# Four activation buffers moved by 8 bytes within each SBUF partition

## The reference

```python
def swiglu(h, w_in, w_out):
    gate, up = jnp.split(h @ w_in, 2, axis=-1)
    return (jax.nn.silu(gate) * up) @ w_out
...
    for l in range(DEPTH):
        x = x + FFN_HALF * swiglu(rmsnorm(x, ffn1_norm[l]), ffn1_w_in[l], ffn1_w_out[l])
        x = x + hybrid_mixer(rmsnorm(x, mix_norm[l]), w_in[l], ...)
        x = x + FFN_HALF * swiglu(rmsnorm(x, ffn2_norm[l]), ffn2_w_in[l], ffn2_w_out[l])
...
    x = x + jnp.sum(gates * proj, axis=2) @ w_o
    x = x + jnp.square(jax.nn.relu(rms_norm(x, g_ffn) @ w_up)) @ w_down
```

## Time and profile before

| | before |
|---|---|
| median of 3 runs | 2320.74 us (2320.18 to 2322.78) |
| the profiled execution | 2317.76 us |
| its span, first to last instruction | 2316.0 us |
| granted TensorE clock, mean | 0.995 of full speed |
| PE busy | 2273.8 us, 98% |
| PEld busy | 2138.2 us, 92% |
| DVE, ACT busy | 1587.5 us (69%), 1404.0 us (61%) |
| DMA | 385.60 MB, mean 166 GB/s |

### The profile page before, as it was taken

One profiled execution on the slowest core, in us unless ns is written; L12 is line 12 of the kernel. 1 busy time (PEld: TensorE's weight loads), 2 busy tenths in 40 slices (PEclk: granted clock), 3 DMA queues, 4 the chain that ended last, 5 costly groups with the idle time before them and its releaser, 6 DMA issues. The chain is left out here.

```text
span 2316.0 us, 40537 instructions
## 1 busy us (share of the span) xinstructions
PE 2273.8 (98%) x17022; PEld 2138.2 (92%) x17022; DVE 1587.5 (69%) x1948; ACT 1404.0 (61%) x1874; POOL 140.9 (6%) x119
## 2 busy tenths in 40 slices
PE   8999999999999999999999999999999999999998
PEld 7998999999999999899989999899989989998997
DVE  5666768856666766667875666679785557978554
ACT  5556788565555655678846655557854445785443
POOL 0000002200000000001300000000040000004000
PEclk9999999999999999999999999999999999999999
DMA  6655444235655565544324465554455655455653
GB/s 222 212 179 187 146 146 146 74 124 168 200 188 194 176 206 181 167 147 145 128 73 146 165 210 176 193 167 141 151 177 188 200 177 182 128 164 171 203 182 127
DMA packets 312452, 385.60 MB, mean 166 GB/s; under 512 B 10812, under 2 KB 287568, under 8 KB 312272
## 3 DMA queue, kind: packets, MB, share of 16 engines
q1 hardware_dynamic: 312160, 382.96, 51.2%
q10 hardware_dynamic: 112, 0.06, 0.0%
HBM read 381.94 MB, written 1.06 MB: 165 GB/s over the span
## 5 line engine op out<-in xcount | busy, mean ns | idle before, releaser
L323 PE MATMUL bank<-xhi,whi 128*128 128x256 f32 x3696 | 1039.5, 281 | 4.5 <-DVE wlo L312 4.1
L324 PE MATMUL bank<-xlo,whi 128*128 128x256 f32 x3696 | 1026.3, 278 | 0.0
L325 PE MATMUL bank<-xhi,wlo 128*128 128x256 f32 x3696 | 1026.0, 278 | 0.0
L301 DVE TENSOR_TENSOR wlo<-raw,whi 128x2048 fp32r<-128x2048 f32 x354 | 816.0, 2307 | 159.2 <-ACT whi L285 153.4
L285 ACT ACTIVATE whi<-raw 128x2048 fp32r<-128x2048 f32 x355 | 676.7, 1907 | 183.5 <-PE bank L325 183.3
L323 PEld LDWEIGHTS bank<-xhi,whi 128*128 128x128 f32 x3696 | 697.6, 189 | 10.2 <-DVE wlo L312 4.2
L324 PEld LDWEIGHTS bank<-xlo,whi 128*128 128x128 f32 x3696 | 696.9, 189 | 5.0 <-issue 1.9
L325 PEld LDWEIGHTS bank<-xhi,wlo 128*128 128x128 f32 x3696 | 696.0, 188 | 0.0
L325 PE MATMUL bank<-whi,ylo 128*128 128x512 f32 x608 | 239.6, 394 | 0.0
L324 PE MATMUL bank<-wlo,yhi 128*128 128x512 f32 x608 | 238.6, 392 | 0.0
L323 PE MATMUL bank<-whi,yhi 128*128 128x512 f32 x608 | 237.1, 390 | 0.6 <-issue 0.6
(11 more groups left out here) (397 smaller groups left out, 2900.5 us busy)
## 6 DMA issues: line engine op xcount, KB each, us to landing
raw<-in_ffn_w_in SPq DMA_DIRECT2D x88, 1024.0 KB, 5.2
raw<-in_w_in SPq DMA_DIRECT2D x88, 1024.0 KB, 5.2
raw<-in_ffn_w_out SPq DMA_DIRECT2D x44, 1024.0 KB, 4.9
raw<-in_w_gate SPq DMA_DIRECT2D x32, 1024.0 KB, 5.7
raw<-in_w_up SPq DMA_DIRECT2D x32, 1024.0 KB, 5.4
raw<-in_w_down SPq DMA_DIRECT2D x32, 1024.0 KB, 4.9
raw<-in_w_branch_b SPq DMA_DIRECT2D x8, 1024.0 KB, 4.9
raw<-in_w_branch_a SPq DMA_DIRECT2D x8, 1024.0 KB, 5.0
```

The costliest lines, as they stand in the source:

```text
L301: e.tensor_tensor(wlo[s][:, 0:size], raw[s][:, 0:size], whi[s][:, 0:size].bitcast(F32), ALU.subtract)\
L323: e.matmul(o, ahi, bhi, start=start, stop=False, skip_group_check=True)
L324: e.matmul(o, ahi, blo, start=False, stop=False, skip_group_check=True)
L325: return e.matmul(o, alo, bhi, start=False, stop=stop, skip_group_check=True)
```

## The change

One buffer, `acts`, takes the place of the four halves. It is 2 words longer than they are together, and the halves are views that begin 2 words (8 bytes) into it. `rstd`, a buffer of 8 bytes, is declared further down, behind `later_keys`.

```diff
-        xhi = sb("xhi", [P, KC, T], F32R)
-        xlo = sb("xlo", [P, KC, T], F32R)
-        yhi = sb("yhi", [P, KC, T], F32R)
-        ylo = sb("ylo", [P, KC, T], F32R)
+        halves_at = sb("acts", [P, 4 * KC * T + 2], F32R)[:, 2:2 + 4 * KC * T].rearrange("p (a c t) -> p a c t", a=4, c=KC)
+        xhi, xlo, yhi, ylo = [halves_at[:, i, :, :] for i in range(4)]
         x = sb("x", [P, TT, D])
         gate_bias = sb("gate_bias", [P, DEPTH * 32])
         lnv = sb("lnv", [P, TT])
-        rstd = sb("rstd", [P, TT])
...
         later_keys = sb("later_keys", [P, 384])
+        rstd = sb("rstd", [P, TT])
```

## The result

The changed kernel takes 2372.67 us (median of 4 runs, 2371.59 to 2374.32) against 2320.93 us for the kernel before in the same comparison: a ratio of 1.0228, 95% interval 1.0216 to 1.0240. The forecast was 2321 us with a range to 2362, so the result lies outside it.

The account below looks back on a forecast made before the run. TensorE, busy 98% of the span, was taken to bound the kernel. Every term was taken as 0, so 2317.8 + 0 us against the profiled execution gave a forecast median of 2321 us, range 2300 to 2362.

Parts of the forecast that it names:

- What bounds the kernel: TensorE, busy 98% of the span: the change can gain or lose only through the distance between matmul starts.
- The distance between the streams: Halves to weight slots, 312 instead of 320 bytes modulo 512: taken as 0, bounds 22 us gained or 39 us added.
- The upper bound, all products slow: Every feature product at 117.7 instead of 113.3 ns, 32 us, plus 7 us for 512-wide row products: 39 us.
- The halves as moving operand: 12,240 matmuls start 8 bytes into a 16-byte unit: taken as 0, at most 1.8 ns each, 22 us.
- 12.6 ns above the columns: 292-wide units, many distances: 134.3 ns per start against 121.7 for columns, read as showing no distance is a disaster.
- Stationary operand: 2,784 matmuls whose weight load touches 33 units instead of 32: cost 0, without cover 5 us.
- Writers: ScalarE and VectorE writing the halves 8 bytes off: cost 0, or 12 us of group time if 10% slower.
- The rest: x, table and arena move by 32 bytes, feeding 1,998 plain fp32 matmuls: cost 0, at 2 ns each 4 us.
- The slow rhythm spreads: Rival: more feature products start 117.7 instead of 113.3 ns apart, 2326 to 2360 us; chance 0.23.
- The quick rhythm spreads: Rival: more feature products start 113.3 instead of 117.7 ns apart, bound 2299 us, half of it 2310; chance 0.26.
- The displaced unit costs on every stream: Rival: 1.8 ns more on each of 12,240 moving streams, 22 us, 2343 us; chance 0.10.
- Half rate: Rival: every 16-byte fetch splits in two, 106.7 ns more for each of 12,240 streams, 3627 us; chance 0.05.

Follow-up runs that it names:

- e2: Against the kernel before, halves begin 16 bytes further, on whole 16-byte units, 304 bytes modulo 512 from the weight slots: 2366.34 us, ratio 1.0201.
- e5: Against the kernel before, halves begin 32 bytes further, 288 bytes modulo 512 from the weight slots: 2359.61 us, ratio 1.0182.
- e6: Against the kernel before, halves begin 64 bytes further, weight slots kept in place, 256 bytes modulo 512 apart: 2363.95 us, ratio 1.0200.
- e11: Against the kernel before, halves stay and all six weight slots move up 16 bytes, distance 336 modulo 512: 2358.78 us, ratio 1.0188.
- e12: Against the kernel before, halves stay and a 128-byte gap ahead of x moves the weight slots, distance 448 modulo 512: 2354.42 us, ratio 1.0168.
- e15: Against the kernel before, halves stay and a 64-byte gap ahead of x moves the weight slots, distance 384 modulo 512: 2364.44 us, ratio 1.0221.
- e16: Against the kernel before, halves stay and the weight slots come 128 bytes down, distance 192 modulo 512: 2352.54 us, ratio 1.0164.
- e10: Against the kernel before, halves and all six weight slots go 8 bytes further, mid-unit, distance still 320: 2396.12 us, ratio 1.0347.
- e9: Against the kernel before, halves and all six weight slots go 16 bytes further, on whole units, distance still 320: 2306.27 us, ratio 0.9958.
- e3: Against the kernel before, halves and five of six weight slots go 8 bytes further, wlo0 32 bytes: 2381.97 us, ratio 1.0271.
- e1: Against the changed kernel, halves begin at the buffer's first word, as before the change; only x, table and arena stay moved by 32 bytes: 2317.48 us, ratio 0.9995.
- e17: Against the kernel before, halves stay and the weight slots come 256 bytes down, distance 64 modulo 512: 2316.81 us, ratio 1.0002.

## Why the prediction was wrong

**What bounds the kernel** was right: TensorE's list sets the end, and the whole change is in the pitch. 65.2 us of busy time became 53.8 us of span.

**The distance between the streams, "I take 0": this step failed.** I argued that the lock re-forms after every disturbance. In the changed kernel a lock does form, 360 ns for three products in 10,368 of 11,652 cases, but it is neither of the two that I knew: which rhythms there are to fall into depends on the distance. With every stream on whole units, seven kernels lose 1.64 to 2.21% (e2, e5, e6, e11, e12, e15, e16), 2352.54 - 2314.89 = 38 us at the least. The upper bound, all products slow, assumed that 117.7 ns is the worst there is; e6 sits at 120 ns. It also rested on a wrong reading of the shares: from rounded durations I had 4 in 10 feature products slow, but by their pitches 2,759 of 11,995 are, about a quarter, and 2,208 row products are 512 wide, not 1,824. With the mean pitches the bound is 12,240 x (117.7 - 114.5) + 2,208 x (233.2 - 229.4) = 39 + 8 = 47 us, 2368 us: still under the 2372.67 measured. e12 and e16, where nearly all products are slow, are 39 and 38 us above before.

**The halves as moving operand, 0 with a bound of 22 us: failed too.** At an unchanged distance, with both streams in the middle of a unit, e10 is 2396.12 - 2306.27 = 90 us slower than e9; its feature products alone, 120.7 against 113.7 ns, make 12,240 x 7.0 = 86 us. The plain fp32 rows did not carry over to fp32r, which the prediction itself had left unsettled, and the bound of 22 us was far too low. The pieces don't add: the change has both causes and is slower by less than e10 has from one. And no layout can part them: the distance of 312 isn't a multiple of 16, so it always leaves one stream off a unit. How the 53.8 us divide between the two stays open. Taking back either one alone leaves most of the loss or more (e2: +2.0%, e3 and e10: +2.7 and +3.5%), and e6, with every stream on a unit, reaches a mean of 119.9 ns against the change's 120.1.

**A row that pointed past my bound** was the earlier trace rows. I read its 12.6 ns above the columns as lying between two known rhythms, and compared it with the row products' 15.9. Set against the feature products, the term in question, it is more than either has: 6.6 and 11.0, or 8.4 in the mean by my shares of 6 to 4. 12,240 x (12.6 - 8.4) = 51 us gives 2369. That is worked out afterwards, and the agreement is luck: those units hold many distances, and with the measured mean before, 114.5 - 106.7 = 7.8, the same sum is 12,240 x (12.6 - 7.8) = 59 us and 2377. But as a bound from the nearest row it belonged in the range.

**The other terms held.** Stationary operand: the 512-wide row products went from 229.4 to 230.8 ns, 3 us, no more than a distance gives without it (e11: 231.1). Writers: 0. The rest: 0 (e1).

**The rivals.** *The slow rhythm spreads* had the sign and the place, and gave 2360 us at most; a rhythm slower than its slow one took its place. *The quick rhythm spreads* is not what the change does, but e9 does it: 2306 us, inside the 2299 to 2321 that this rival allowed. *The displaced unit costs on every stream* expected the two old rhythms 1.8 ns longer, about 115 and 119; both were gone. *Half rate* would have shown 213 ns, which no kernel has. The last sentence of the prediction, that I would be most wrong if a third rhythm appeared, is what happened.

Of the two pages that I weighed, both speak for no change, and the measurement decides against that here. The Trainium skill (SBUF — State Buffer, the note on SBUF cachelines) asks for two hits on a 16-byte line, which the first and last lines of e10's streams have; e10 still loses. It also says (TensorE: Matmul & The Clock Gate, Part 2) that the read ports of the moving operand and of the weight load are independent; by that a distance could do nothing, and e12 and e16 against e17 show that it does, by 1.6%.

What stays open: why a distance of 64 modulo 256 is quick, and why a stream that starts off a unit is slow. The runs show both as facts of addresses. A period of 256 bytes rests on two pairs of distances, and no distance but 320 was tried at more than one common shift.

## What to carry to other kernels

Where TensorE is 98% busy, look at the pitch of its matmuls and how it varies between stretches with the same operands: two values mean that something beside the columns counts, and that addresses may move it. Then keep fp32r operands on whole 16-byte units (every kernel here with the halves off one was 2.3 to 3.5% slower), and treat the distance modulo 256 bytes between the moving operand and the stationary one as a parameter to try: here it spans 2306 to 2366 us on whole units. When a row shows more overhead than the known cases, let the range reach there.

## What the runs showed of the hardware that I had not expected

- At a granted clock of 1.00, products of 256 fp32r columns with a weight load each fall into fixed rhythms in ten of the twenty kernels: three of them take 340, 353 to 354 or 360 ns in 89 to 98% of the cases (113.3, 117.8 and 120.0 ns each in the mean, against 106.7 for the columns). In the other ten kernels only 3 to 45% do, and the pitches are mixed.
- Which of them occur depends on the distance between the two operands in their partitions, modulo 256 bytes as far as two pairs show it: 64 and 320 give means of 114.4 and 114.5 ns, 192 and 448 both give 117.6.
- A moving fp32r operand that starts 4 or 8 bytes into a 16-byte unit means 120.1 to 121.9 ns at the four distances tried (312, 316, 320 and 328).
- At the quick distance a common shift of 16 bytes (e9) cuts the pitches of 117 to 119 ns from 2,759 to 571, and the kernel is 0.42% quicker.
